# Seven RMS norms summed by a matrix of 1/1024 and rooted on whole 128x512 blocks, with three small steps moved ahead of a weight split

## What is computed

```python
def rmsnorm(x, g):
    y = x32 * lax.rsqrt(jnp.mean(x32 * x32, axis=-1, keepdims=True) + EPS)
    return (y * g)

def first_block(x, ...):
    h = swiglu(rmsnorm(x, norm_ffn1_pre), w_ffn1_in, w_ffn1_out)
    x = x + 0.5 * rmsnorm(h, norm_ffn1_post)
    h = mixer(rmsnorm(x, norm_mix_pre), w_mix_in, ...)
    x = x + rmsnorm(h, norm_mix_post)
    h = swiglu(rmsnorm(x, norm_ffn2_pre), w_ffn2_in, w_ffn2_out)
    x = x + 0.5 * rmsnorm(h, norm_ffn2_post)
    return x

def hybrid_layer(x, c, norm_gain, ...):
    mod = silu(c) @ w_ada + b_ada
    h = rms_norm(x, norm_gain) * (1.0 + scale) + shift
    ...            # attention, pooling, two branches, w_out
    return x + gate * out
# and rms_norm(x, final_gain) at the very end
```

## Time and profile before

| | |
|---|---|
| median of 3 runs | 1606.37 us (1605.62 to 1607.95) |
| profiled execution, its own time | 1609.75 us |
| its span (first to last instruction) | 1608.1 us |
| mean granted TensorE clock | 0.98 of full |
| PE busy | 1551.2 us (96% of the span) |
| DVE, ACT, POOL busy | 801.1, 585.5, 209.4 us |

### The profile page before, as it was taken

One profiled execution on the slowest core, in us unless ns is written; L12 is line 12 of the kernel. 1 busy time (PEld: TensorE's weight loads), 2 busy tenths in 40 slices (PEclk: granted clock), 3 DMA queues, 4 the chain that ended last, 5 costly groups with the idle time before them and its releaser, 6 DMA issues.

```text
span 1608.1 us, 18797 instructions
## 1 busy us (share of the span) xinstructions
PE 1551.2 (96%) x7157; PEld 1280.5 (80%) x7157; DVE 801.1 (50%) x890; ACT 585.5 (36%) x783; POOL 209.4 (13%) x228
## 2 busy tenths in 40 slices
PE   7999999997999998999999999799999999999997
PEld 6888888885887886788888887688888877888876
DVE  3434434326366745543344233777888865433244
ACT  5222222223465413422222223466666633222222
POOL 4555455103110002000000000100000000000001
PEclk9999999998899998999999999799999999999999
DMA  5544444231142231322322322022122232332321
GB/s 173 157 143 150 137 151 149 94 101 53 53 115 73 79 105 53 105 87 95 104 92 92 105 104 78 27 79 77 54 78 64 67 105 82 102 105 79 103 79 53
DMA packets 136071, 152.91 MB, mean 95 GB/s; under 512 B 3248, under 2 KB 123180, under 8 KB 136028
## 3 DMA queue, kind: packets, MB, share of 16 engines
q1 hardware_dynamic: 131580, 137.40, 27.1%
q0 software_dynamic: 4304, 14.88, 3.3%
q10 hardware_dynamic: 144, 0.04, 0.0%
HBM read 150.08 MB, written 2.23 MB: 95 GB/s over the span
## 4 chain that ended last, share of the span: by engine, by line
PE 62%; DVE 2%; POOL 1%; ACT 1%; issue 1%; POOLq 0%; ACTq 0%; DVEq 0%
PE ps L1572 19%; PE ps L1574 19%; PE ps L1573 19%; PE ps L1849 1%; POOL xT L530 1%; PE ps L1859 1%; PE ps L1832 1%; PE ps L1858 1%; PE ps L1831 1%; DVE acc L1048 1%; PE ps L1636 0%; POOL xT L585 0%; PE ps L1768 0%; DVE tt L1067 0%; PE ps L1833 0%
## 5 line engine op out<-in xcount | busy, mean ns | idle before, releaser
L1572 PE MATMUL ps<-ah,wh 128*128 128x512 f32 x1504 | 601.3, 400 | 15.9 <-DVE al L1040 9.3
L1574 PE MATMUL ps<-ah,wl 128*128 128x512 f32 x1504 | 590.1, 392 | 0.0
L1573 PE MATMUL ps<-al,wh 128*128 128x512 f32 x1504 | 589.3, 392 | 0.0
L1007 DVE TENSOR_TENSOR wl<-raw,wh 128x2048 fp32r<-128x2048 f32 x94 | 215.3, 2290 | 402.6 <-ACT wh L602 402.3
L602 ACT ACTIVATE wh<-raw 128x2048 fp32r<-128x2048 f32 x94 | 179.9, 1914 | 482.2 <-PE ps L1574 482.2
L1572 PEld LDWEIGHTS ps<-ah,wh 128*128 128x128 f32 x1504 | 285.5, 190 | 73.3 <-issue 11.6
L1574 PEld LDWEIGHTS ps<-ah,wl 128*128 128x128 f32 x1504 | 284.4, 189 | 60.5
L1573 PEld LDWEIGHTS ps<-al,wh 128*128 128x128 f32 x1504 | 285.0, 190 | 55.5
L1572 PE MATMUL ps<-rh,wh 128*128 128x512 f32 x352 | 136.9, 389 | 0.0
L1573 PE MATMUL ps<-rl,wh 128*128 128x512 f32 x352 | 136.9, 389 | 0.0
L1574 PE MATMUL ps<-rh,wl 128*128 128x512 f32 x352 | 136.9, 389 | 0.0
(11 more groups left out here) (284 smaller groups left out, 1690.4 us busy)
## 6 DMA issues: line engine op xcount, KB each, us to landing
raw<-in_w_ffn_in SPq DMA_DIRECT2D x43, 1024.0 KB, 5.1
raw<-in_w_ffn_out SPq DMA_DIRECT2D x22, 1024.0 KB, 4.8
raw<-in_w_in SPq DMA_DIRECT2D x36, 512.0 KB, 4.8
raw<-in_w_in SPq DMA_DIRECT2D x14, 1024.0 KB, 5.9
ada_raw<-in_w_ada POOLq DMA_DIRECT2D x24, 512.0 KB, 4.6
raw<-in_w_mix_in SPq DMA_DIRECT2D x10, 1024.0 KB, 5.3
raw<-in_w_mix_out SPq DMA_DIRECT2D x4, 1024.0 KB, 4.9
raw<-in_w_branch_a SPq DMA_DIRECT2D x4, 1024.0 KB, 4.9
```

The costliest lines, as they stand in the source:

```text
L1007: nc.vector.tensor_tensor(wl[n % 2][:], raw[n % 2][:], wh[n % 2][:].bitcast(fp32), ALU.subtract).then_inc(lo_done, 1)
L1572: nc.tensor.matmul(bank, w[0], m[0], start=start, stop=False)
L1573: nc.tensor.matmul(bank, w[0], m[1], start=False, stop=False)
L1574: return nc.tensor.matmul(bank, w[1], m[0], start=False, stop=stop)
```

## The change

For stages 0 to 6, a new constant matrix mean (128x128, all 1/1024) is the stationary operand of full fp32 matmuls of 128x512: acc once, and then each square that is not in acc. The result is the mean over the channels, already on all partitions. ScalarE takes the root of the whole 128x512 block out of PSUM, with eps as its bias, and VectorE takes the reciprocal of the whole block in place (rstd). The spread, the 128x4 steps and the copy to rstd go. A table ADDS says how many squares are added into acc: 6 of them as before in stages 0, 2, 4, then 5 in stages 1, 3, 5 (so TensorE multiplies acc and two squares there), and none in stage 6 (TensorE multiplies all eight squares). Stage 7 stays as it was. Besides, the split of the gate weights (gates_hi, gates_lo), the copy of the first bank (h7) and the loading of ScalarE's root table stand ahead of the split of the next weight slot. GpSimd gets two more memsets at the start. The new function of VectorE, the new sums of TensorE and the table, with the calls:

```diff
-        ACC = {stage: 6 * stage - 3 * (stage > 6) for stage in range(8)}
+        ADDS = (6, 5, 6, 5, 6, 5, 0, 6)
+        ACC = {stage: sum(ADDS[:stage]) for stage in range(8)}
...
+            nc.gpsimd.memset(eps1[:], EPS)
             nc.gpsimd.memset(ones[:], 1.0)
+            nc.gpsimd.memset(mean[:], 1.0 / D)
...
-            def root(stage):
-                act.wait_ge(var_done, stage + 1)
-                nc.scalar.activation(r4[:], r4[:], ACT.Sqrt).then_inc(rstd_done, 1)
+            def root(stage, bank):
+                act.wait_ge(sum_done, stage + 1)
+                nc.scalar.activation(rstd[:], ps[:, bank, :], ACT.Sqrt, bias=eps1[:]).then_inc(rstd_done, 1)
...
             def post_norm(stage, o, last):
-                load_root(o)
...
                 hi(base_out + 10)
                 unit(10)
+                first()
                 hi(base_out + 11)
...
+            def gates_hi():
+                load_root(0)
+                act.wait_ge(gpad, 1)
...
-            def variance(stage, bank, spread=True):
-
-                dve.wait_ge(sum_done, stage + 1)
-                chain.link(nc.vector.tensor_scalar(r4[:], ps[:, bank, 0:TB], 1.0 / D, EPS, ALU.mult, ALU.add))
-                nc.vector.reciprocal(r4[:], r4[:]).then_inc(var_done, 1)
-                dve.wait_ge(*((rb_done if spread else rstd_done), stage + 1))
+            def inverse_root(stage):
+
+                dve.wait_ge(rstd_done, stage + 1)
+                chain.link(nc.vector.reciprocal(rstd[:], rstd[:]))
...
-                for j in range(1, 7):
+                for j in range(1, ADDS[stage] + 1):
...
-                chain.link(nc.vector.tensor_copy(rstd[:], ps[:, 7, :]))
...
-                        variance(stage, 4)
-                        chain.link(nc.vector.tensor_copy(rstd[:], ps[:, 4, :]))
+                        inverse_root(stage)
...
                 lo(base_out + 10)
                 unit(10)
+                first()
                 lo(base_out + 11)
...
             def sums(stage, bank):
 
+                adds = ADDS[stage]
+                if adds:
+                    pe.wait_ge(acc_step, ACC[stage] + adds)
+                    nc.tensor.matmul(ps[:, bank, :], mean[:], acc[:], start=True, stop=False)
+                for j in range(adds + 1 if adds else 0, KD):
+                    pe.wait_ge(sq_done, 8 * stage + j + 1)
+                    source = sq[:, j % 2, :] if adds else sq6(j)
+                    last = nc.tensor.matmul(ps[:, bank, :], mean[:], source, start=j == 0, stop=j == KD - 1)
+                last.then_inc(sum_done, 1)
...
-                    elif k == 6:
-                        spread(stage, 4)
```

More of the change, by code:

```diff
@@ L65 @@
 MIXER = [(0, "qk", {0: [("gates",), ("ada", 0)], 1: [("ada", 1)], 2: [("ada", 2)], 3: [("ada", 3)], 4: [("ada", 4), ("sums",)],
-                    5: [("ada", 5)], 6: [("ada", 6), ("spread",)], 7: [("ada", 7), ("rows", 0)]}),
+                    5: [("ada", 5)], 6: [("ada", 6), ("norm",)], 7: [("ada", 7), ("rows", 0)]}),
          (0, "v", {3: [("rows", 1)]}),
@@ L655, in post_norm, with ffn @@
                 squares(stage, ready, banks=True)
-                root(stage)
-            def ffn(f, stage, base_in, base_out):
+                root(stage, 7)
+            def ffn(f, stage, base_in, base_out, first):
                 def unit(j, i=0):
@@ L668, in pair @@
                     if isinstance(i, int) and i == 0:
-                        root(stage)
+                        root(stage, 4)
                     for j in units:
@@ L709, in _ @@
             load_root(3)
[L710 to L716, removed]
+            def gates_hi():
+                load_root(0)
+                act.wait_ge(gpad, 1)
+                act.wait_ge(gates_in, 16 * 5)
+                for q in range(4):
+                    last = nc.scalar.activation(gh[:, :, 32 * q:32 * q + HEADS], gw[:, :, HEADS * q:HEADS * q + HEADS], ACT.Copy)
+                last.then_inc(gw_hi, 1)
+            ffn(0, 0, S_F1I, S_F1O, gates_hi)
             post_norm(1, 0, S_MIX - 1)
@@ L730, in mixer_step @@
             def mixer_step(kind, *step):
-                if kind == "spread":
-                    root(2)
+                if kind == "norm":
+                    root(2, 4)
                 elif kind == "rows" and step[0] == 0:
@@ L1155, in _, with gates_lo @@
             lo(1)
[L1156 to L1162, removed]
+            def gates_lo():
+                dve.wait_ge(gw_hi, 1)
+                for q in range(4):
+                    cols = slice(32 * q, 32 * q + HEADS)
+                    last = nc.vector.tensor_tensor(gl[:, :, cols], gw[:, :, HEADS * q:HEADS * q + HEADS],
+                                                   gh[:, :, cols].bitcast(fp32), ALU.subtract)
+                last.then_inc(gw_lo, 1)
+                first_bank(0, S_MIX - 1)
+            ffn(0, 0, S_F1I, S_F1O, gates_lo)
             post_norm(1, 0, S_MIX - 1, "norm_ffn1_post", 1, after=lambda j: scaled_lo(j, 1, "norm_mix_pre"))
@@ L1174, in mixer_step @@
                     nc.vector.tensor_tensor(gmod[:], gmod[:], par[:, col["norm_gain_2"]:col["norm_gain_2"] + 8], ALU.mult).then_inc(mod_done, 1)
-                elif kind == "spread":
-                    variance(2, 4)
-                    chain.link(nc.vector.tensor_copy(rstd[:], ps[:, 4, :]))
+                elif kind == "norm":
+                    inverse_root(2)
                     chain.link(nc.vector.tensor_tensor(rsq, rstd[:], rstd[:], ALU.mult))
@@ L1559, in _ @@
             gained(KD - 1)
-            variance(7, 7, spread=False)
+            dve.wait_ge(sum_done, 8)
+            chain.link(nc.vector.tensor_scalar(r4[:], ps[:, 7, 0:TB], 1.0 / D, EPS, ALU.mult, ALU.add))
+            nc.vector.reciprocal(r4[:], r4[:]).then_inc(var_done, 1)
+            dve.wait_ge(rstd_done, 8)
             for n in OUT_DVE:
@@ L1621, in last_slot, with token_sums @@
                 before()
[L1622 to L1625, removed]
-            def sums(stage, bank):
+                if whole_bank:
+                    token_sums()
+                    whole_bank(6)
+                    whole_bank(7)
+                else:
+                    sums(stage, 7)
+            def sums(stage, bank):
+                adds = ADDS[stage]
[7 more added lines that the diff above has]
+                last.then_inc(sum_done, 1)
+            def token_sums():
+                stage, bank = 7, 7
                 for step in range(2):
@@ L1800, in _ @@
             last_slot(S_F2I - 1, (ah[:, 2:4, :], al[:, 2:4, :]), R_MO + 4, 1, 3, lambda: pe.wait_ge(h7_done, 2))
-            spread(3, 7)
             ffn(1, 2, 4, S_F2I, S_F2O, 2)
             pe.wait_ge(t_done, 8 * T_OF[5] + 3)
[L1808 to L1818, removed]
+            sums(6, 4)
             def att_step(step, r):
```

38 lines of the change are left out of this document (18 added, 20 removed).

## The result

The changed kernel takes 1625.43 us (median of 4 runs, 1624.88 to 1628.46); the kernel before took 1607.16 us on the same chip. The ratio is 1.0115, with a 95% interval of 1.0095 to 1.0135: slower by 1.15%. The prediction was 1611 us, range 1595 to 1616; the sign was right, the size was not, and the range missed it. The profiled execution of the changed kernel took 1624.88 us, 15.1 more than the profiled one of before.

A forecast was written before the change was run, and what follows sets the result against it. TensorE, busy 96% of the span, was taken to bound the kernel. Stages added 6.8 us to the median 1606.4, less 2.5 of the 5.1 us clock gain: 1611 us, range 1595 to 1616.

The forecast's parts named there:

- stage 0, gap before the third slot: TensorE's third slot waits for gt behind VectorE's reciprocal and starts at 44.05 instead of 43.22; plus 0.8 us.
- stage 1: Post norm: mean matmuls, root and reciprocal delay GpSimd's residual adds from 388.00 to 389.7; plus 1.7 us.
- stage 2, clock: Mixer's first slot: mean matmuls replace one-column sums, so the clock holds; minus 5.1 us in the profiled execution.
- stage 3: Post norm with the same steps as stage 1, 633.9 against 632.30; plus 1.6 us.
- stage 4: Third slot waits for gt behind the reciprocal, until 662.45; plus 0.4 us.
- stages 5 and 6: Last post norms: a second reciprocal, almost paid for by dropped serial adds and one-column matmuls; together plus 2.3 us.
- The reciprocal at "3.3 us": VectorE on 128x512: time grows with the elements, 3.3 us, bounds 0.7 and 4.8; forecast's 2.9 to 3.8 had chance 0.40.
- The mean matmul at "0.92 us": TensorE, fp32 128x512: priced from 129-column fp32 matmuls at 0.231 us each, 0.92 us; other end 0.45.
- Rival A: VectorE's reciprocal runs at the plain rate, 0.7 us, making the kernel faster: 1597 us, range 1594 to 1600; chance 0.30.
- Half of the fall, 2.5 us: Stage 2: the clock may not fall in every run, so 2.5 us of the 5.1 counted against the median.
- "The rest.": Two memsets delay the first transposes by under 0.2 us, the h7 copy a weight split by about 0.2; both covered.
- all four: Rivals: reciprocal 0.7, 1.3 to 2.5 or 3.9 to 4.8 us, or mean matmul 0.45; chances 0.30, 0.12, 0.10, 0.08.

The follow-up runs named there:

- placed: Changed kernel with spare tensor room 96 bytes instead of 128, so tensors behind it begin at multiples of 64 bytes again; 1614.51 us, ratio 1.0034 to the kernel before.
- before_stage2: Kernel before with stage 2 alone done the new way (two mean matmuls, root and reciprocal, no spread); 1604.94 us, ratio 0.9974.
- placed_unmoved: placed with the moves undone (gate split, copy of bank 7 and root table back behind the last weight split); 1614.20 us.
- placed_lnexp: placed with root and reciprocal of the seven norms replaced by exp(-0.5 ln(x)) on ScalarE; 1602.80 us, ratio 0.9962 to the kernel before.
- placed_onetable: placed_lnexp with activation table set 6 loaded by an explicit instruction ahead of the norms; 1595.05 us, ratio 0.9916 to the kernel before.
- before_shifted: Kernel before with spare tensor room 160 bytes instead of 128, so tensors behind it begin 32 bytes off a multiple of 64; 1619.79 us, ratio 1.0062.
- before_ah32: Kernel before with ah and al alone moved to 32 bytes off a multiple of 64 by two unused tensors; 1630.54 us, ratio 1.0137.
- before_moved: Kernel before with only the moves (gate split, copy of bank 7, root table ahead of the next weight split); 1606.65 us, ratio 0.9990.

## Why the prediction missed

Its terms, with what the trace of placed shows against that of before (starts of the same matmul in both), in us:

| step | predicted | measured, placed against before |
|---|---|---|
| stage 0, gap before the third slot | +0.8 | +0.5 (+1.0 in the changed kernel), and +1.7 of low clock behind it |
| stage 1 | +1.7 | +1.6 |
| stage 2, clock | -5.1 | -5.2 at 425 us, -4.9 at 490 us, with the spread's time in it |
| stage 3 | +1.6 | +1.6 |
| stage 4 | +0.4 | +0.6 |
| stages 5 and 6 | +2.3 | +2.1, and +0.9 of low clock behind them |
| where the other tensors lie | no term | +10 (changed kernel against placed) |

*Prices.* The reciprocal at "3.3 us" was right (3.35), and so was its reason, that the 178 ns row grows with the elements. It was also luck in part: the rows of before left everything from 0.7 to 4.8 us open, as the prediction says, and its choice had a chance of 0.40. The mean matmul at "0.92 us" took 0.86, the root at "0.72" took 0.69. The measured (3.35 - 0.155) / 512 is 6.2 ns an element.

*The norms, stages 0 to 6.* The step by step sum holds to 0.3 us a stage. Rival A's sum holds to 3 us too: with a cheap operation in that place the kernel is at 1600.

*Stage 2.* The clock held in the changed kernel and in placed, as "I expect the clock to hold" said. That the sums have to do with it is borne out by before_stage2, whose nine runs lie 3.9 us lower in the median and closer together; placed_unmoved shows that they are not all of it. Half of the fall, 2.5 us, was counted against the median, which was too little by 1.4.

*"The rest."* This is the step that failed. It costed the two new tensors by their memsets and nothing else. Their 544 bytes moved everything allocated behind them to 32 bytes off a multiple of 64, and that costs 10.9 us between the medians. Without it the kernel takes 1614.5 us, inside the range of 1595 to 1616, and slower than before by 0.34%; so the sign was right for the reason given, and about two thirds of the measured slowdown had another cause. No rival held that cause either, because all four were about the price of new operations.

*A smaller miss, of size.* The sum took gaps at their own length. Behind the gaps in stages 0 and 6, TensorE ran at a granted clock of 0.50 for longer than before, 2.6 us together in the profiled run of placed. A further fall in placed, from 492 to 500 us (granted 0.82 and 0.75, 1.6 us), comes after work that both kernels have. The changed kernel's own run has one from 460 to 463 us instead, and placed_lnexp has neither; what decides it stays open. So does the mechanism in the chip that makes a 64-byte boundary matter to a matmul's stream; the runs show the cost and what it hangs on, no more. Whether a single instruction can make the inverse root was not tried.

## What to carry to other kernels

An edit that allocates something, however small, moves what is allocated behind it: compare the starting addresses of the streamed operands before and after, and look at the mean duration of matmuls that the edit does not touch. Price a reciprocal by its elements, not by its instruction: on 4 elements a partition it took 0.18 us, on a whole block of 512 it took 3.35 and was the longest step of a norm, and exp(-0.5 ln(x)) from one table set did the work of root and reciprocal in 1.34 us (382.23 to 383.57 in placed_onetable). After pricing each gap, ask what the clock does behind it, and compare several runs before giving the clock's share to the edit.

## What was not expected of the hardware

- An fp32r matmul of 128x512 whose streamed operand begins 32 bytes off a multiple of 64 takes 0.2333 us from start to start instead of 0.2267 (3%), and its record 395 or 396 ns instead of 389. The runs show it for rh in two kernels (changed, before_shifted) and for ah in a third (before_ah32), and in each of them what lay at a multiple of 64 kept 389.
- VectorE's reciprocal takes 178 ns on 4 elements and 3352 ns on 512, five times a plain tensor_tensor (0.69 us).
- The activation table was loaded twice for Ln and Exp side by side (1.28 us each, 14 loads for the seven norms of placed_lnexp) until one set, number 6, was loaded explicitly ahead of the norm; then none stood at either of them (placed_onetable).
- The granted clock fell to 0.50 for 10 us while TensorE was busy all the time, behind 16 one-column records of the sums and the like ones of ada ahead of them (the profiled runs of before and before_moved). With the same sums it stayed up in before_shifted, and with two full-width matmuls in place of the sixteen it stayed up in seven profiled runs and fell in one (placed_unmoved, ahead of the sums).
